# Attention and retention of a two-layer encoder step: copies, waits and banks rearranged between ScalarE, VectorE and TensorE

## The reference

```python
# layer 0, mixer A (8 heads, keys chosen by an indexer) and mixer B (8 heads, latent keys)
qb = (rmsnorm(cqlat, g_qlat) @ w_uq).reshape(nb, t, B_HEADS, B_NOPE + B_ROPE)
qn = rmsnorm(qb[..., :B_NOPE], g_qn)
qr = rope(rmsnorm(qb[..., B_NOPE:], g_qr), pos)
p = jax.nn.softmax(s, axis=-1)
o = jnp.einsum('bhqs,bshd->bqhd', p, v.astype(F32))
# layer 1, mixer D (4 heads of retention)
o = jnp.einsum('bihd,bjhd->bhij', q, k) * decay[None]
o = jnp.einsum('bhij,bjhe->bihe', o, v)
o = o + jnp.einsum('bihd,bhde->bihe', q, s) * inter[None, :, :, None]
od = rmsnorm(od.astype(u.dtype), g_dn).reshape(nb, t, D_HEADS * D_VDIM) * jax.nn.silu(dg)
```

## Time and profile before

| | |
|---|---|
| median of 3 runs | 2869.35 us (2869.24 to 2869.51) |
| profiled execution | 2871.04 us, its span 2869.1 us |
| PE busy | 2851.2 us, 99% of the span |
| DVE busy | 1428.7 us, 50% |
| ACT busy | 1070.8 us, 37% |
| POOL busy | 186.4 us, 6% |
| read from memory | 396.48 MB, 140 GB/s over the span |

### The profile page before, as it was taken

One profiled execution on the slowest core, in us unless ns is written; L12 is line 12 of the kernel. 1 busy time (PEld: TensorE's weight loads), 2 busy tenths in 40 slices (PEclk: granted clock), 3 DMA queues, 4 the chain that ended last, 5 costly groups with the idle time before them and its releaser, 6 DMA issues.

```text
span 2869.1 us, 45023 instructions
## 1 busy us (share of the span) xinstructions
PE 2851.2 (99%) x18666; PEld 2806.6 (98%) x18666; DVE 1428.7 (50%) x1546; ACT 1070.8 (37%) x1236; POOL 186.4 (6%) x112
## 2 busy tenths in 40 slices
PE   9999999999999999999999999999999999999999
PEld 9997799999999999999999999899999999999999
DVE  7677645543443343344466774546444443444443
ACT  5334533332332233233335633434333333333332
POOL 2000002000000000000221241112000000000000
PEclk9999999999999999999999999999999999999999
DMA  6433024444444444444444444244444444444443
GB/s 232 138 114 110 30 89 140 143 143 140 146 141 141 145 140 141 145 140 141 145 148 155 152 148 148 95 162 147 149 153 147 154 147 152 150 149 153 147 152 136
DMA packets 112783, 405.25 MB, mean 141 GB/s; under 512 B 12656, under 2 KB 14752, under 8 KB 112480
## 3 DMA queue, kind: packets, MB, share of 16 engines
q1 hardware_dynamic: 108864, 392.64, 41.1%
q0 software_dynamic: 1616, 6.31, 0.6%
q10 hardware_dynamic: 2128, 3.66, 0.3%
HBM read 396.48 MB, written 6.09 MB: 140 GB/s over the span
## 4 chain that ended last, share of the span: by engine, by line
PE 97%; DVE 2%; ACT 1%; issue 0%; DMA 0%; ACTq 0%; DVEq 0%
PE PS L1411 31%; PE PS L1416 30%; PE PS L1415 30%; PE PS L1490 0%; ACT pr L483 0%; DVE pr L910 0%; DVE w_lo L843 0%; PE PS L1691 0%; DVE rb L1052 0%; PE PS L1488 0%; PE PS L1866 0%; PE PS L1474 0%; ACT w_hi L435 0%; PE PS L1738 0%; PE PS L1737 0%
## 5 line engine op out<-in xcount | busy, mean ns | idle before, releaser
L843 DVE TENSOR_TENSOR w_lo<-stage,w_hi 128x1024 fp32r<-128x1024 f32 x734 | 920.3, 1256 | 1197.0 <-ACT w_hi L435 1196.6
L435 ACT ACTIVATE w_hi<-stage 128x1024 fp32r<-128x1024 f32 x740 | 784.6, 1061 | 1634.3 <-PE PS L1416 1624.9
L1411 PE MATMUL PS<-xh,w_hi 128*128 128x336 f32 (+1 forms) x3264 | 1025.1, 314 | 1.0 <-DVE kk L1087 0.6
L1416 PE MATMUL PS<-xh,w_lo 128*128 128x336 f32 (+1 forms) x3248 | 1017.1, 313 | 0.0
L1415 PE MATMUL PS<-xl,w_hi 128*128 128x336 f32 (+1 forms) x3248 | 1015.6, 313 | 0.0
L1411 PE MATMUL PS<-hh,w_hi 128*128 128x336 f32 (+1 forms) x2032 | 635.7, 313 | 0.0
L1416 PE MATMUL PS<-hh,w_lo 128*128 128x336 f32 (+1 forms) x2032 | 635.0, 313 | 0.0
L1415 PE MATMUL PS<-hl,w_hi 128*128 128x336 f32 (+1 forms) x2032 | 634.1, 312 | 0.0
L1411 PEld LDWEIGHTS PS<-xh,w_hi 128*128 128x128 f32 x3264 | 613.1, 188 | 3.5 <-issue 1.1
L1415 PEld LDWEIGHTS PS<-xl,w_hi 128*128 128x128 f32 x3248 | 612.5, 189 | 0.4
L1416 PEld LDWEIGHTS PS<-xh,w_lo 128*128 128x128 f32 x3248 | 610.0, 188 | 0.0
(11 more groups left out here) (343 smaller groups left out, 1529.1 us busy)
## 6 DMA issues: line engine op xcount, KB each, us to landing
stage<-in_wstream SPq DMA_DIRECT2D x740, 512.0 KB, 3.3
out_s<-so POOLq DMA_DIRECT2D x8, 256.0 KB, 2.8
x<-in_x_in SPq DMA_DIRECT2D x6, 336.0 KB, 7.1
out_y<-x ACTq DMA_DIRECT2D x3, 672.0 KB, 3.9
dmask<-in_ret POOLq DMA_DIRECT2D x4, 352.0 KB, 5.7
stage<-in_wstream SPq DMA_DIRECT2D x4, 256.0 KB, 3.7
s<-in_s_in POOLq DMA_DIRECT2D x1, 1024.0 KB, 6.2
x<-in_x_in SPq DMA_DIRECT2D x4, 168.0 KB, 3.9
```

Of the source, the lines that this page charges most:

```text
L435: act.activation(w_hi[:, s, :], stage[:, s, :], ACT.Copy).then_inc(hi_ready, 1)
L843: dve.tensor_tensor(w_lo[:, s, :], stage[:, s, :], w_hi[:, s, :].bitcast(F32), ALU.subtract).then_inc(lo_ready, 1)
L1411: pe.matmul(out, wh, rh, start=first, stop=False)
L1416: mm = pe.matmul(out, wl, rh, start=False, stop=last)
```

## The change

1. **Second query projection.** DVE copies the four banks one by one (four instructions for one), and PE's next chunk waits for each bank alone. The rotary part's multiplication (L1183) moves behind the third copy. `query_sums` starts with the rotary heads, which need one third of the squares, and waits for the others as it comes to them; DVE fetches the two sums apart.
2. **Attention.** Both copies to `ptb` move from DVE to ACT, and ACT makes `pta` and `ptb` ahead of the exponentials of its step. DVE makes `mol` one step later. In A, DVE normalises head 1 already at step 1, ahead of the fetch of the sums; the roots are taken at the start of ACT's step 8 and their ratio at step 8 of DVE. Half of `keys_b(0)` moves to PE's step 8, ahead of its transposes.
3. **Retention.** Odd heads use banks 1 and 2 as before, even heads banks 6 and 7, for the turned tokens and for the output; `osq2` is a second buffer of squares. `retained` waits no more for the normalisation of the head before. The mask of head h+1 moves on DVE ahead of the wait for the root of head h. On ACT, the high part of head h moves into the turn of head h+1, behind its six token copies (`round_output`).

```diff
-                act.wait_ge(od_ready, h + 1)
-                act.activation(moh[:, 8 + 2 * h:10 + 2 * h, LIVE], z2[:, DG + 2 * h:DG + 2 * h + 2, LIVE],
-                               ACT.Copy).then_inc(doh_ready, 1)
...
+                b = out_bank(h)
+                act.activation(squares_of(h)[:, :, LIVE], PS[:, b:b + 2, LIVE], ACT.Square).then_inc(osq_ready, 1)
                 if h < 3:
                     tokens_first(h + 1)
+                if h:
+                    round_output(h - 1)
                 act.wait_ge(oms_psum, h + 1)
...
                 if h < 3:
                     state_queries(h + 1)
+                if h < 3:
+                    decayed_scores(h + 1)
                 dve.wait_ge(osd_ready, h + 1)
                 ch.link(dve.reciprocal(osd[:, LIVE], osd[:, LIVE]))
-                if h < 3:
-                    decayed_scores(h + 1)
...
             def retained(h):
 
-                if h:
-                    pe.wait_ge(on_ready, 2 * h)
-                else:
+                if h == 0:
                     pe.wait_ge(s0_in_s, 16)
+                pe.wait_ge(ktok_ready, h + 1)
...
                     if g0 == 0 and s == 1:
+                        weights(1)
                         dve.wait_ge(qb_ms, 1)
-                        dve.tensor_copy(sdq[0:8], PS[0:8, 4:6, 0:T]).then_inc(qb_taken, 1)
...
+                        dve.tensor_copy(sdq[0:8, 1], PS[0:8, 5, 0:T])
+                        dve.wait_ge(qb_ms, 2)
+                        dve.tensor_copy(sdq[0:8, 0], PS[0:8, 4, 0:T]).then_inc(qb_taken, 1)
...
-                    dve.tensor_copy(qb[:, 4 * c:4 * c + 4, :], PS[:, 4:8, 0:T]).then_inc(qkv_evac, 1)
+                    for o in range(4):
+                        dve.tensor_copy(qb[:, 4 * c + o, :], PS[:, 4 + o, 0:T]).then_inc(qkv_evac, 1)
...
-                pe.wait_ge(qkv_evac, 3)
-                pe.wait_ge(qb_sq, 3)
+                pe.wait_ge(qkv_evac, 10)
+                pe.wait_ge(qb_sq, 1)
```

More of the change, by code:

```diff
@@ L375, in build, with squares_of, out_bank @@
         CD_COLS = [ALL, ALL, LIVE, LIVE, ALL, ALL, LIVE, LIVE, ALL, ALL, LIVE, LIVE]
+        def squares_of(h):
+            return osq2 if h % 2 else osq
+        def out_bank(h):
+            return 1 if h % 2 else 6
         def SB(n):
@@ L477, in attend @@
                 for s in range(8 + 3):
+                    if g0 == 0 and s == 8:
+                        softplus_input()
+                        act.wait_ge(qb_taken, 1)
+                        act.activation(sdq[0:8], sdq[0:8], ACT.Sqrt, bias=gcol("eps", rows=slice(0, 8))
+                                       ).then_inc(qb_sd, 1)
+                    if 2 <= s < 10:
+                        g = g0 + s - 2
+                        act.wait_ge(pt_psum, g + 1)
+                        if g >= 2:
+                            act.wait_ge(o_psum, g - 1)
+                        act.activation(pta[:, g % 2], PS[:, pb, :].rearrange("p (a b) -> p a b", a=4),
+                                       ACT.Copy).then_inc(pta_ready, 1)
+                        act.activation(ptb[0:80, g % 2, 0:80], PS[0:80, pb + 1, 0:80], ACT.Copy)
+                        act.activation(ptb[NS_TOK:80, g % 2, 80:T], PS[NS_TOK:80, pb + 1, 80:T],
+                                       ACT.Copy).then_inc(ptb_ready, 1)
                     if s < 8:
@@ L1403, in _, with product @@
         def _(pe):
-            def product(u, j, kt, rh, rl, first, last, bank0, m=4, cols=ALL):
+            def product(u, j, kt, rh, rl, first, last, bank0, tiles=range(4), cols=ALL, free=None):
                 s = u % NR
-                for o in range(m):
+                for o in tiles:
+                    if free:
+                        free(o)
                     c = 512 * j + P * o
@@ L1445, in sum_squares, with attend @@
                 return f
-            def attend(g0, scores, values, sb, tail):
+            def attend(g0, scores, values, sb, fill, tail):
                 pb, ob = 4 - sb, 6 - sb
@@ L1459, in attend @@
                         query_sums()
+                    if s >= 8:
+                        fill(s)
                     if 2 <= s < 10:
@@ L1634, in _ @@
                         kt = 2 * k + j
-                        mm = product(u, j, kt, qlath[:, kt, :], qlatl[:, kt, :], kt == 0, kt == 3, 4)
+                        mm = product(u, j, kt, qlath[:, kt, :], qlatl[:, kt, :], kt == 0, kt == 3, 4,
+                                     free=bank_free if c and kt == 0 else None)
                     mm.then_inc(unit_done, 1)
@@ L1710, in _ @@
             key_sums(0)
-            keys_b(1)
+            keys_b(1, range(4))
             pe.wait_ge(mol_ready, 8)
@@ L1742, in _ @@
             attend(8, scores_b, lambda h, k: vB[:, k, P * h:P * h + P], 4,
-                   lambda s: chunk(U_ABOUT, G_ABOUT, moh, mol, ks=(s - 8,), need=need_heads))
+                   lambda s: chunk(U_ABOUT, G_ABOUT, moh, mol, ks=(s - 8,), need=need_heads), lambda s: None)
             chunk(U_ABOUT, G_ABOUT, moh, mol, ks=range(3, CU), need=need_heads)
@@ L1863, in retained @@
                 for e in range(2):
-                    bank = 1 + e
+                    bank = out_bank(h) + e
                     c = P * e
@@ L1881, in output_squares @@
                 for e in range(2):
-                    mm = pe.matmul(PS[:, 0, LIVE], ones, osq[:, e, LIVE], start=e == 0, stop=e == 1)
+                    mm = pe.matmul(PS[:, 0, LIVE], ones, squares_of(h)[:, e, LIVE], start=e == 0, stop=e == 1)
                 mm.then_inc(oms_psum, 1)
```

111 lines of the change are left out of this document (54 added, 57 removed).

## The result

The changed kernel takes 2875.09 us (median of 19 runs, 2873.53 to 2878.30), the kernel before 2869.81 us (19 runs, 2868.83 to 2875.75): a ratio of 1.0014, with a 95% interval of 1.0007 to 1.0020, some 4 us slower. The medians lie 5.3 us apart, the means 4.2, since the kernel before has a long upper side: ten of its runs took 2868.83 to 2869.81 us, the other nine 2870.55 to 2875.75. The profiled execution took 2873.59 us with a span of 2871.8 us, against 2871.04 and 2869.1 before.

A forecast was written before the change was run, and what follows sets the result against it. PE, busy 99% of the span, was taken as the bound. Query part 0, A -4.4, B -1.2, retention +8.1 sum to +2.5 us; on the before median of 2869.35 that gives 2871.8 us, range 2866.5 to 2877.

The forecast's parts named there:

- The query part: Second query projection and `query_sums`: 2.7 us gained, given back as a 2.8 us wait before A's first transposes; sum 0.
- the 0.2 us that I took: Query projection: extra time per set of four split copies on DVE, at 0.42 us a quarter.
- Attention A: ACT copies first, later waits go: 1.3 + 3.2 - 0.15, a gain of about 4.4 us.
- I allow 0.15 us: Attention A, ACT's step 8: loss for two small instructions, table load and root before head 6's copy, covered by half of `keys_b(0)`.
- Attention B: The 1.07 us wait before the transposes goes, with 0.15 us of hidden end: gain 1.2 us.
- The retention: 4.8 us gained, two new 4.8 us waits at `output_squares` cost 9.6 us, low clock 3.3 us: +8.1 us.
- the clock stays up in the retention: Rival: no clock fall behind the retention's new waits; -0.8 us, 2868.5, or 2870.2 with one fall; chance 0.25.
- no wait for `so`: Rival, retention: DVE has head 1's state before PE asks; -10.4 us, 2859; chance 0.06.
- the gain of A does not come: Rival: first two steps or ACT's longer turn eat it; A gives 1.3 us or so; +5.6 us, 2875; chance 0.07.
- I let these 1.66 us go: Retention: slower PE work after the first `retained` wait, 4.99 against 3.33 us, counted as gained with that wait.
- The rival of the clock in A: Clock also falls behind A's new 2.8 us wait, up to 1.66 us, or stays low longer: 2874 to 2877.5; chance 0.14.

The follow-up runs named there:

- e7_both: e6 with head 1's normalisation in attention A put back behind the fetch of the sums: 2861.25 us, ratio 0.9965 to the kernel before.
- e10_no_fill: e6 with the work ahead of step 8's transposes (piece of `keys_b(0)`; in B of the output product) put back behind them: 2867.87 us, ratio 0.9989 to before.
- e1_round_back: Changed kernel with ScalarE's high part of a retention head back at the end of that head's own turn: 2864.58 us, ratio 0.9979 to before.
- e3_retention: Kernel before with the retention's part of the change alone: 2879.50 us, ratio 1.0031 to before.
- e4_filled_wait: Changed kernel with 36 unread identity transposes ahead of `output_squares` of heads 1 and 2: 2870.82 us, ratio 1.0002 to before.
- e2_attention: Kernel before with the query projection's and attention's part of the change alone: 2866.55 us, ratio 0.9986 to before.
- e6: Changed kernel with the rounding moved ahead of the token copies, right behind ScalarE's copy of the state: 2862.82 us, ratio 0.9973 to before.
- e11_state_first: e7_both with VectorE's `so` of the next head put ahead of `mol`: 2860.07 us, ratio 0.9962 to the kernel before.
- e8_filled_a: e6 with 25 unread identity transposes in the wait before attention A's first transposes: 2861.79 us, ratio 0.9967 to before.

## Why the prediction was right, and where it was off

**The query part** went as reckoned. Four quarter copies step 1.67 us together where one copy stepped 1.47, the 0.2 us that I took:

```profile
269.12 1.75 DVE L1225 COPY qb<-PS 128x336 f32<-128x336 f32 x4
270.79 1.22 DVE L862 TENSOR_TENSOR w_lo<-stage,w_hi 128x1024 fp32r<-128x1024 f32 x1
```

The 0.375 us by the Trainium skill (VectorE: DVE Perf Modes, "The TRN2 errata") is not borne out here: the three more instructions cost 0.2 us. The first transposes stand at 281.66 (said: 281.55) behind 2.81 us (said: 2.8). That the fetch of the sums sets this start is shown by e7_both, which has the fetch before head 1's normalisation and waits 1.45 us instead of 2.80.

**Attention A** gained 3.9 us from its first transposes on, not 4.4. The second transposes came 0.25 us later than said, 0.11 of it because the first did; the `ptb` copies step 0.23 and 0.40 us, not 0.2 and 0.3. The step that was mis-sized is "I allow 0.15 us" for step 8: it is 0.54. A table load and the root (1.28 and 0.85 us) now stand ahead of `pta` there, and e10_no_fill shows that their cover, half of `keys_b(0)`, is worth 2.3 us of wait: without it most of A's gain would have gone.

**Attention B**, with all that stands from `rope_spreads` to the retention, gained 1.46 us (1.2 said). I had overlooked that the output product's first chunk moves ahead of step 8's transposes in B too; by e10_no_fill that changes nothing.

**The retention** came out at +7.96 us (+8.1 said): two waits of 4.57 us (4.8), and 3.8 us of low clock (3.3). e1_round_back and e3_retention show the cause, the place of the rounding, and e4_filled_wait that the clock's share is 3.6 us. The rivals "the clock stays up in the retention", "no wait for `so`" and "the gain of A does not come" are excluded.

**The base of the sum.** By spans the change costs 2.7 us, as predicted (2.5). By the ratio it costs 4.0 us, by the medians 5.3: the median is 2875.09, 3.3 us above the forecast, and the range holds it only because its upper side was drawn for slower rivals. The step that failed is "I let these 1.66 us go": I took the low clock of the earlier trace rows off, and then set the sum on the median, which is 1.69 us below that execution. The same wait in e2_attention had no fall. Without this credit the sum is +4.2 us; with the 1.1 us or more of A's clock, below, it reaches the 5.3 of the medians. That most executions of before have no fall is borne out by the mean clock of each run. Beside the experiments the kernel before ran 63 times: 37 runs list 1.000 and took 2868.95 to 2870.97 us, 26 list 0.999 or 0.998, as the profiled one does, and took 2870.77 to 2874.62. In which stage the clock fell in those is not shown, as runs without a profile list no stretch of clock.

**The rival of the clock in A** did come, beside the forecast, not instead of it. With the 2.8 us wait the clock fell in six of seven profiled executions, and A was then 1.1 to 2.5 us longer (30.39 to 31.83 against 29.31, e1, e4, e6 and e2). The profiled execution of the changed kernel was the one without, and it lies 1.5 us below its median. I gave this rival 0.14 together with a longer fall in the retention; it deserved more, since I had a row for a fall behind half that wait.

The Trainium skill (TensorE: Matmul & The Clock Gate, "What's actually happening") says of the clock's rise that its moment varies from run to run with the monitor's phase. If the same holds for its fall, which no run here shows, that would fit a fall behind 2.8 us in six executions of seven and behind 1.4 us in one retention and not in another.

## What to carry to other kernels

An instruction that is put behind others on one engine also delays what the next engine has queued behind its consumer: follow the chain to the far end (here `moh`, `mol`, `so`, `output_squares`) before calling the delay hidden, and keep it ahead of the block. Here its old place turned 8 us of loss in the retention into 3.5 of gain (1.7 of them a low clock in the profile before), and the place early in the next turn gave 0.2 more. A wait on TensorE has two prices, its length and the clock behind it; the second differs between executions, so a term read from one execution must not be taken off a median; the mean clock of the runs tells whether they are like the profiled one. Where a wait can't be removed, work that nobody reads in it can give back the second price, without moving anything else.

## What the runs showed of the hardware

- Clock: behind 4.57 us the clock fell every time (four of four, changed and e3_retention), behind 2.8 us in six of seven, behind 2.89 us in A in the one profile that has such a wait (e10_no_fill), behind the waits of 1.40 and 1.41 us in the retention in one of four (before and e2_attention), and in none of two behind 1.45 us in A (e7_both and e11_state_first). 4.1 us of small transposes in the wait kept it at 1.00 (e4_filled_wait), and so did 2.9 us of them in A (e8_filled_a).
- VectorE's product of 128x640 over SBUF takes 0.82 us alone. Beside GpSimd's product of 128x1280 it takes 2.84 us (2.11 us in the kernel before, where it began 1.46 us after GpSimd's), and both times it ends 0.69 us after GpSimd's does: it hardly advances while that runs. The Trainium skill (Advanced Engine Details and Errata, "GPSIMD Details") states that GpSimd shares a read and a write interface with VectorE and conflicts with VectorE instructions that have two SBUF inputs. This product has two, and the rows agree.
- ScalarE copies from PSUM 80 columns on 80 partitions in 0.22 us and 256 columns on 16 partitions in 0.38 us, steps of 0.23 and 0.40 us.
